# A second accumulator, two pool regions and moved gate and SiLU steps in a diffusion trunk layer

## The chip, the cores and the metric

The kernel runs on one core of a Trainium2 chip. TensorE (PE) multiplies, VectorE (DVE), ScalarE (ACT) and GpSimd (POOL) do the rest, and SyncE (SP) issues the DMAs; each works through its own queue in order, and semaphores join them. The metric is the device time of one execution in microseconds; lower is better. Three runs of the kernel before gave a median of 1373.22 us (1372.56 to 1376.62).

## What is computed

One layer of a trunk for 1024 latent tokens (a grid of 16 rows of 64) and 128 context tokens, model width 1024, float32:

```python
ada = jax.nn.silu(cond) @ p['w_ada'] + p['b_ada']
sh1, sc1, g1, sh2, sc2, g2 = jnp.split(ada, 6, axis=-1)
h = modulate(layer_norm(x), sh1, sc1)
proj = h @ p['w_in']
...
pool_out = pool_mixer(xp.reshape(B, rows, cols, POOL_W), p['w_pool'], p['pool_scale']).astype(x.dtype)
ml_out, st_new = mlstm_mixer(q, k, v, o, gates, p['w_qk_conv'], p['b_gates'], p['hn_g'], st0)
mix = jnp.concatenate([pool_out, ml_out], axis=-1) @ p['w_out']
x = layer_norm(ALPHA * x + g1[:, None, :] * mix, p['ln1_g'], p['ln1_b'])
h = modulate(layer_norm(x), sh2, sc2)
ffn = conv_ffn(h, rows, cols, p['w_up'], p['w_dw'], p['b_dw'], p['w_down'])
x = layer_norm(ALPHA * x + g2[:, None, :] * ffn, p['ln2_g'], p['ln2_b'])
```

The pooling mixer takes, in four groups of 128 channels, means over windows of 2, 4, 8 and 16 in both grid directions, subtracts the input and multiplies each group by a 128 x 128 matrix and a scale. The mLSTM mixer convolves q and k over three tokens, applies SiLU, and scans chunks of 128 tokens forwards and backwards with gates that come from 16 further columns of the projection.

## The kernel before

Each engine has one program. This case is about the stretch from 93 us to 345 us: the input projection and the first step of the scan.

**Units.** The projection up to the scan has 16 tiles of 128 output columns: four of the pooling input, then four of v, of q and of k; four more tiles, of the output gate, follow in units 32 to 39. A tile is two units (halves of the contraction) `n`; a unit is three groups `g` of 384 tokens, each of 12 matmuls, so 36 matmuls. Every weight block is split into a rounded part `whi` (ACT, `hi(n)`) and a rest `wlo` (`lo(n)`: DVE up to unit 25, POOL from unit 26 on), and three products are summed. The two buffers of `whi` and `wlo` alternate, so `hi(n + 2)` waits until unit `n` is done, and PE starts unit `n` when `lo(n)` is done. Tiles 8 to 15 (units 16 to 31) are q and k: when a tile is complete, ACT copies it out of PSUM, DVE adds the two outer taps of the convolution (`conv(j)`, line 2668, four instructions), and ACT applies SiLU (`silu(j)`, line 1729).

**Between the units.** PE's loop over `n` has small jobs in it. `ada2_cols(j)` (line 1145, its matmuls in line 1113) turns modulation block `j` of six into columns in PSUM bank 6. A block is summed by DVE in eight `ada_unit`s of two instructions (lines 2684 and 2686) into the one accumulator `aacc`; the first unit of block `j` waits until the columns of block `j - 1` have been read. The table `ADA_UNITS` says which unit of the projection is followed by how many of them, and `ADA_COLS` follows from it: block 0 is read in unit 5, block 1 in 11, block 2 in 19, block 3 in 27, 4 in 29, 5 in 31, after group 0 of that unit. The gate jobs `gT`, `grow`, `mcol` and `tok` (lines 1212 to 1226) alternate with DVE's `gate_chain1` to `gate_chain5`. After units 10 to 21 one job of four transposes (line 1236) turns v into rows, through PSUM bank 7, and ACT copies it out (`v_evac`, line 1746); after units 24 to 29 come twelve `pool_job`s (line 1248), which multiply the pooled channels by `w_pool`, each into the same columns of bank 7. ACT scales the result into the tile `po` (`po_evac`, line 1723), rounds it to `pohi` (line 1725), POOL forms `polo` (`po_lo`), and SP writes both to DRAM (`spill_pool`). `po_evac(j)` waits for the `polo` of `j - 1`, since `po` is one tile, and from `j = 3` on also for the spill of `j - 3`.

**The pooling mixer** itself, window means of the four groups, is a chain of instructions on POOL (lines 2206 to 2251). It starts when `gate_chain4` is done, and pool job 0 is copied out when it has ended (`pool_y`).

**SP** issues in program order, for each `n`: the block of unit `n + 4`, the loads of `adaw` (two `ada_unit`s to a pair, two buffers, each load waits for the pair before last), then the spills. In the scan, `O_SLOTS` says at which of three places (a, b, c) of a step PE does one group of the output gate's projection.

## Time and profile before

| | |
|---|---|
| median of three runs | 1373.22 us |
| the profiled execution | span 1374.0 us |
| PE busy | 1276.8 us, 93% of the span |
| DVE busy | 1026.9 us, 75% |
| POOL busy | 674.8 us, 49% |
| ACT busy | 589.6 us, 43% |
| PE's waits between 93 us and 345 us | 19.6 us in 9 waits of 0.5 us or more |

The span runs from the first to the last instruction of the profiled execution; the page gives no other time of it. Busy PE is not PE at its peak, since the end of a matmul is modelled.
### The profile page before, as it was taken

How to read it: one execution, taken by the hardware profiler on the slowest of the kernel's cores; microseconds unless marked ns; L12 is line 12 of the kernel's file. 1: busy time of each engine (PE TensorE's matmuls, PEld its weight loads, DVE VectorE, ACT ScalarE, POOL GpSimd, SP SyncE). 2: the span in 40 equal slices, each digit the busy share in tenths (PEclk: the TensorE clock that was granted, in tenths of full speed). 3: DMA queues.
4: the chain of work that ended last, by engine and by line, in shares of the span. 5: the costliest groups of instructions: out<-in, count | busy, mean ns of one | idle time of the engine just before them, and what ended most of it. 6: DMA issues, size and time to landing. Idle time of an engine off the chain costs nothing.

```text
span 1374.0 us, 21762 instructions
## 1 busy us (share of the span) xinstructions
PE 1276.8 (93%) x7739; PEld 1181.1 (86%) x7739; DVE 1026.9 (75%) x1510; ACT 589.6 (43%) x1019; POOL 674.8 (49%) x507
## 2 busy tenths in 40 slices
PE   5899899988999699998799999999999999999995
PEld 3689899878898677898799999999999988888884
DVE  7565669674566688879977778877875689878698
ACT  5442123444435625544344444444443455445420
POOL 1001999333333131227968787978786974300011
PEclk9899899999999799999899999999999999999998
DMA  9432221364235243111253545345444479955774
GB/s 341 144 93 85 66 85 46 107 212 114 82 85 206 84 171 108 62 62 31 90 187 114 189 152 166 134 155 178 141 161 144 158 249 330 351 165 184 239 255 195
DMA packets 164339, 210.28 MB, mean 153 GB/s; under 512 B 10567, under 2 KB 101795, under 8 KB 164003
## 3 DMA queue, kind: packets, MB, share of 16 engines
q1 hardware_dynamic: 163774, 204.47, 45.1%
q0 software_dynamic: 288, 4.72, 0.9%
q8 instruction: 46, 0.75, 0.2%
q14 instruction: 34, 0.28, 0.1%
q10 hardware_dynamic: 197, 0.06, 0.0%
HBM read 161.49 MB, written 47.72 MB: 152 GB/s over the span
## 4 chain that ended last, share of the span: by engine, by line
PE 77%; DVE 10%; issue 3%; ACT 3%; POOL 3%; DMA 3%; SPq 0%; DVEq 0%; POOLq 0%; ACTq 0%
PE ps L1202 12%; PE ps L1548 10%; PE ps L1546 10%; PE ps L1547 10%; PE ps L1581 5%; PE ps L1580 5%; PE ps L1579 5%; PE ps L1154 2%; DMA adaw<-in_w_ada 1%; PE ps L1422 1%; PE ps L1113 1%; PE ps L1424 1%; PE ps L1423 1%; DVE qk L2668 1%; PE ps L1330 1%
## 5 line engine op out<-in xcount | busy, mean ns | idle before, releaser
L2980 DVE SCALAR_TENSOR_TENSOR ps<-gs,taps,ps 128x945 f32<-128x945 f32 (+2 forms) x176 | 215.8, 1226 | 56.9 <-ACT ps L1956 51.5
L1202 PE MATMUL ps<-h1hi,whi 128*128 128x384 f32 x432 | 154.6, 358 | 0.0
L1202 PE MATMUL ps<-h1lo,whi 128*128 128x384 f32 x432 | 147.1, 341 | 0.0
L1202 PE MATMUL ps<-h1hi,wlo 128*128 128x384 f32 x432 | 147.1, 340 | 0.0
L2321 POOL TENSOR_TENSOR rstd<-mv,neghalf 128x1 f32<-128x1 f32 x27 | 27.5, 1018 | 242.1 <-DVE mv L3154 161.5
L1579 PE MATMUL ps<-dwhi,uhi 128*128 128x512 f32 x290 | 113.0, 390 | 1.3 <-POOL dwlo L2173 1.3
L1581 PE MATMUL ps<-dwhi,ulo 128*128 128x512 f32 x290 | 112.8, 389 | 0.0
L1580 PE MATMUL ps<-dwlo,uhi 128*128 128x512 f32 x290 | 112.8, 389 | 0.0
L1546 PE MATMUL ps<-thi,xhi 128*128 128x288 f32 x320 | 96.9, 303 | 8.6 <-issue 5.2
L1548 PE MATMUL ps<-thi,xlo 128*128 128x288 f32 x320 | 96.5, 302 | 0.0
L1547 PE MATMUL ps<-tlo,xhi 128*128 128x288 f32 x320 | 96.5, 302 | 0.0
L2173 POOL TENSOR_TENSOR wlo<-raw,whi 128x512 fp32r<-128x512 f32 x46 | 67.8, 1477 | 56.4 <-ACT whi L1651 27.0
L1546 PE MATMUL ps<-thi,whi 128*128 128x288 f32 x320 | 94.2, 294 | 0.7 <-POOL wlo L2173 0.7
L1548 PE MATMUL ps<-thi,wlo 128*128 128x288 f32 x320 | 94.4, 295 | 0.0
L1547 PE MATMUL ps<-tlo,whi 128*128 128x288 f32 x320 | 94.2, 294 | 0.0
L2686 DVE SCALAR_TENSOR_TENSOR aacc<-adaw,colv,aacc 128x512 f32<-128x512 f32 x84 | 88.9, 1098 | 2.8 <-DMA adaw<-in_w_ada 2.2
L1202 PEld LDWEIGHTS ps<-h1hi,whi 128*128 128x128 f32 x432 | 83.2, 193 | 2.0 <-issue 0.2
L1202 PEld LDWEIGHTS ps<-h1lo,whi 128*128 128x128 f32 x432 | 83.3, 193 | 1.7 <-issue 0.2
L1651 ACT ACTIVATE whi<-raw 128x512 fp32r<-128x512 f32 x42 | 26.3, 628 | 133.9 <-PE ps L1202 132.8
L1202 PEld LDWEIGHTS ps<-h1hi,wlo 128*128 128x128 f32 x432 | 83.0, 192 | 0.0
L1548 PE MATMUL ps<-h2hi,wlo 128*128 128x288 f32 x240 | 71.5, 298 | 0.0
L1546 PE MATMUL ps<-h2hi,whi 128*128 128x288 f32 x240 | 71.4, 297 | 0.0
(425 smaller groups left out, 3998.9 us busy)
## 6 DMA issues: line engine op xcount, KB each, us to landing
raw<-in_w_up SPq DMA_DIRECT2D x78, 256.0 KB, 4.6
u_rows<-val SPq DMA_DIRECT2D x22, 576.0 KB, 2.9
adaw<-in_w_ada SPq DMA_DIRECT2D x24, 512.0 KB, 3.9
st<-in_w_down SPq DMA_DIRECT2D x22, 512.0 KB, 4.4
t_rows<-st SPq DMA_DIRECT2D x11, 1024.0 KB, 5.0
raw<-in_w_in SPq DMA_DIRECT2D x40, 256.0 KB, 4.1
w_raw<-in_w_down SPq DMA_DIRECT2D x33, 256.0 KB, 4.9
v_raw<-u_rows SPq DMA_DIRECT2D x33, 256.0 KB, 4.7
```

What stands on the lines that cost most here:

```text
L1154: last = mm(ps[:, 3 * tile + g, 0:GN], a[:, n % 2, k * P:(k + 1) * P], b[:, kk, grp(g)], start=(kk == 0 and a is whi and b is h1hi), stop= ...
L1202: last = mm(ps[:, bank, 0:GN], a[:, n % 2, k * P:(k + 1) * P], b[:, kk, grp(g)], start=(kk == 0 and a is whi and b is h1hi), stop=(kk == K ...
L1546: mm(out, hi_w[:, ks], b_hi[:, k, cols], start=(n < 2 and k == 0), stop=False, skip_group_check=True)
L1547: mm(out, hi_w[:, ks], b_lo[:, k, cols], start=False, stop=False, skip_group_check=True)
L1548: last = mm(out, lo_w[:, ks], b_hi[:, k, cols], start=False, stop=(k == KH - 1), skip_group_check=True)
L1579: mm(out, u_hi, w_hi, start=start, stop=False, skip_group_check=True)
L1580: mm(out, u_hi, w_lo, start=False, stop=False, skip_group_check=True)
L1581: return mm(out, u_lo, w_hi, start=False, stop=stop, skip_group_check=True)
L2173: return nc.gpsimd.tensor_tensor(out, full, hi_part.bitcast(F32), ALU.subtract)
L2321: tt(rstd[:, j % 4, :], mv[:, j % 4, 1:2], neghalf[:, 0, :], ALU.pow).then_inc(rstd_ready, 1)
L2686: last = stt(out, src, s_col, out, ALU.mult, ALU.add)
L2980: step(stt(a3[:, ro, co], g3[:, ri, ci], taps[:, tap:tap + 1], a3[:, ro, co], ALU.mult, ALU.add), 2 + m)
```

## The change

It does these things:

- A second accumulator `aacc_side`, where no live data lie once two small tables of the gates have been written to DRAM, takes blocks 3 and 5 of the modulation. The first unit of blocks 3, 4 and 5 then waits for the columns of one block earlier than before.
- `ADA_UNITS` has a unit more after projection units 21 and 23 and one less after 27 and 28, so block 3 is read in unit 26 instead of 27.
- The columns of all six blocks are read after group 1 of their unit instead of group 0; from unit 26 on PE waits there until ACT has copied out all pool jobs that lie in bank 6.
- Pool jobs alternate between bank 7 and columns 128 to 511 of bank 6, and `po` is two tiles. A pool job waits for the copy of the job before last, and ACT's copy for the `polo` of the job before last. ACT waits for the spill behind that copy, no longer ahead of it.
- `gate_chain5` moves on DVE from after the units of `n = 9` to ahead of them.
- `silu(j)` moves on ACT from the end of an odd `n` to the end of the even `n` that follows.
- The first group of unit 33 moves from place b of scan step 0 to ahead of the scan.

```diff
-ADA_UNITS = {..., 19: 1, 21: 1,
-             23: 1, 24: 3, 25: 3, 26: 3, 27: 4, 28: 4, 29: 3}
+ADA_UNITS = {..., 19: 1, 21: 2,
+             23: 2, 24: 3, 25: 3, 26: 3, 27: 3, 28: 3, 29: 3}
+ADA_SIDE = (3, 5)
...
-O_SLOTS = {0: "abc", 1: "ac", ...}
+O_SLOTS = {0: "ac", 1: "ac", ...}
...
-        po = place("po", [P, GN], work_at + 4 * 2 * T + 4 * H * P)
+        po = [place("po0", [P, GN], work_at + 4 * 2 * T + 4 * H * P), place("po1", [P, GN], past_xt + 1600)]
...
+        aacc_side = place("aacc_side", [P, 2, AC], tmp_at + 4 * 4 * AC + 8 * AC)
...
+        def ada_sum(blk):
+            return aacc_side if blk in ADA_SIDE else aacc
+
+        def pool_bank(j):
+            return ps[:, 7, 0:GN] if j % 2 == 0 else ps[:, 6, P:P + GN]
...
-                acc_cols(6, 2 * (4 + j) * AB, [aacc[:, w, :] for w in both]).then_inc(pe_ada, 1)
+                acc_cols(6, 2 * (4 + j) * AB, [ada_sum(j)[:, w, :] for w in both]).then_inc(pe_ada, 1)
...
-                if j:
-                    pe.wait_ge(po_ready, j)
-                mm(ps[:, 7, 0:GN], wpl[:, g, :], qk[:, H + g, grp(part)], start=True, stop=True).then_inc(pe_pool, 1)
+                if j >= 2:
+                    pe.wait_ge(po_ready, j - 1)
+                mm(pool_bank(j), wpl[:, g, :], qk[:, H + g, grp(part)], start=True, stop=True).then_inc(pe_pool, 1)
...
-                    if g == 0 and n in ADA_COLS:
+                    if g == 1 and n in ADA_COLS:
+                        if n > POOL_FIRST:
+                            pe.wait_ge(po_ready, min(2 * (n - POOL_FIRST), 12))
                         ada2_cols(ADA_COLS[n])
...
             for g in range(NG):
                 o_unit(U_C, g)
+            o_groups = [(n, g) for n in range(U_C + 1, U_OUT) for g in range(NG)]
+            o_unit(*o_groups.pop(0))
...
                 if j == 0:
                     act.wait_ge(pool_y, 4)
-                else:
-                    act.wait_ge(polo_ready, j)
+                elif j >= 2:
+                    act.wait_ge(polo_ready, j - 1)
+                fn(po[j % 2][:, :], pool_bank(j), ACT.Copy, scale=colv[:, V_PS + g:V_PS + g + 1]).then_inc(po_ready, 1)
+                act.wait_ge(po_ready, j + 1)
                 if j >= 3:
                     act.wait_ge(po_out[r], 32 * g)
-                fn(po[:, :], ps[:, 7, 0:GN], ACT.Copy, scale=colv[:, V_PS + g:V_PS + g + 1]).then_inc(po_ready, 1)
-                act.wait_ge(po_ready, j + 1)
-                fn(pohi[:, r, :], po[:, :], ACT.Copy).then_inc(pohi_ready, 1)
+                fn(pohi[:, r, :], po[j % 2][:, :], ACT.Copy).then_inc(pohi_ready, 1)
...
-                    if 2 * H < tile < NPROJ - 1:
-                        silu(tile - 2 * H - 1)
+                elif 2 * H < n // 2 - 1 < NPROJ - 1:
+                    silu(n // 2 - 2 - 2 * H)
...
                 if kk == 0:
-                    dve.wait_ge(pe_ada, N_ADA1 + blk)
+                    dve.wait_ge(pe_ada, N_ADA1 + (blk if blk < ADA_SIDE[0] else blk - 1))
+                    if blk == ADA_SIDE[0]:
+                        dve.wait_ge(rows_out, 32)
...
-                if n == 10:
-                    gate_chain5()
...
+                if n == 9:
+                    gate_chain5()
                 for unit in range(ada_done(n - 1), ada_done(n)):
                     ada_unit(unit)
```

Line numbers in the order of the changed kernel are 7 to 13 higher than before.

DVE's queue around units 9 and 10. Before, the four instructions on `aacc` (`ada_unit` 14 and 15) stand ahead of `gate_chain5` (the copies into `tok` and `decb`); `wlo<-raw,whi` are `lo(11)` and `lo(12)`:

```order
L2523 TENSOR_TENSOR wlo<-raw,whi 128x512
L2686 SCALAR_TENSOR_TENSOR aacc<-adaw,colv,aacc 128x512 x4
L2645 COPY tok<-ps 128x128
L2646 TENSOR_SCALAR tok<-ps 128x128
L2647 COPY tok<-ps 128x128
L2648 COPY decb<-ps 128x128
```

The same place of the changed kernel:

```order
L2533 TENSOR_TENSOR wlo<-raw,whi 128x512
L2655 COPY tok<-ps 128x128
L2656 TENSOR_SCALAR tok<-ps 128x128
L2657 COPY tok<-ps 128x128
L2658 COPY decb<-ps 128x128
L2661 MEMSET v_75 128x36
L2698 SCALAR_TENSOR_TENSOR aacc<-adaw,colv,aacc 128x512 x4
```

The gate chain has passed the four accumulator instructions.

ACT's queue at units 19 to 21: `whi<-raw` are `hi(21)` and `hi(22)`, the two copies out of `ps` are tile 9, `v_75<-ps` are copies of v, and line 1729 is `silu(0)`. Before:

```order
L1651 ACTIVATE whi<-raw 128x512
L1780 ACTIVATE qk<-ps,colv 128x1152
L1782 ACTIVATE work<-ps 128x1152
L1729 ACT_TABLE_LOAD
L1729 ACTIVATE qk<-qk 128x1152
L1746 ACTIVATE v_75<-ps 128x4x128
L1651 ACTIVATE whi<-raw 128x512
L1746 ACTIVATE v_75<-ps 128x4x128
```

And in the changed kernel:

```order
L1661 ACTIVATE whi<-raw 128x512
L1790 ACTIVATE qk<-ps,colv 128x1152
L1792 ACTIVATE work<-ps 128x1152
L1756 ACTIVATE v_75<-ps 128x4x128
L1661 ACTIVATE whi<-raw 128x512
L1739 ACT_TABLE_LOAD
L1739 ACTIVATE qk<-qk 128x1152
L1756 ACTIVATE v_75<-ps 128x4x128
```

The SiLU now stands behind the next copy of v and the next rounding.

PE's queue in unit 5, with row numbers: the first row each time is the last matmul ahead of the columns of block 0, and line 1113 (1121) is that read. Before:

```order
257 L1202 MATMUL ps<-h1hi_71,wlo_51 128x384
258 L1113 MATMUL ps<-pick_59,aacc_107 128x2 x8
259 L1202 MATMUL ps<-h1hi_71,whi_50 128x384
260 L1202 MATMUL ps<-h1lo_72,whi_50 128x384
261 L1202 MATMUL ps<-h1hi_71,wlo_51 128x384
```

In the changed kernel:

```order
269 L1210 MATMUL ps<-h1hi_71,wlo_51 128x384
270 L1121 MATMUL ps<-pick_59,aacc_108 128x2 x8
271 L1210 MATMUL ps<-h1hi_71,whi_50 128x384
272 L1210 MATMUL ps<-h1lo_72,whi_50 128x384
273 L1210 MATMUL ps<-h1hi_71,wlo_51 128x384
```

The read stands 12 matmuls, one group, later; the `grow` job behind it is row 307 in both.

## Rows read from the trace of the kernel before

**Rows 1.** The page: its first line; the adaw loads: KB each, us to landing.

```profile
span 1374.0 us, 21762 instructions
...
adaw<-in_w_ada SPq DMA_DIRECT2D x24, 512.0 KB, 3.9
```

**Rows 2.** Waits of PE, 93 to 345 us: us in total, times, longest.

```profile
PE ps L1248 <- ACT po L1723: 7.0, 3, 3.5
PE ps L1236 <- DVE decb L2648: 3.9, 1, 3.9
PE ps L1113 <- DVE aacc L2686: 3.5, 1, 3.5
PE ps L1236 <- ACT v L1746: 3.0, 1, 3.0
PE ps L1292 <- ACT qk L1729: 1.0, 1, 1.0
PE ps L1305 <- ACT kw L1812: 0.7, 1, 0.7
```

**Rows 3.** Windows after two waits: length, busy times, granted clock, DMA share, GB/s.

```profile
145.00:158.50 13.50, 13.50 (x58) 13.47 (x59) 5.13 (x4) 0.60 (x1) 12.86 (x12) 0.62 0.27 78
279.00:284.00 5.00, 4.35 (x14) 3.70 (x13) 4.96 (x6) 3.52 (x5) 2.68 (x2) 0.66 0.92 308
```

**Rows 4.** Timelines of PE and DVE, units 5 and 6: start, duration, instruction, idle before.

```profile
101.77 1.84 PE L1113 MATMUL ps<-pick,aacc 128*128 128x2 f32 x16
...
112.18 0.60 PE L1217 MATMUL ps<-ident,gcol 128*1 128x128 f32 x4
...
103.72 0.88 DVE L2684 TENSOR_SCALAR aacc<-adaw,colv 128x512 f32<-128x512 f32 x2 [2.59 <-PE ps L1113]
...
111.96 0.17 DVE L2611 MEMSET mrow<- 1x128 f32 x1
```

**Rows 5.** Timeline of DVE, unit 10.

```profile
135.77 8.26 DVE L2686 SCALAR_TENSOR_TENSOR aacc<-adaw,colv,aacc 128x512 f32<-128x512 f32 x4
```

**Rows 6.** Timeline of ACT, unit 20.

```profile
220.71 1.16 ACT L1729 ACTIVATE qk<-qk 128x1152 f32<-128x1152 f32 x1 [3.69 <-DVE qk L2668]
```

**Rows 7.** Timeline of DVE, units 18 to 24.

```profile
205.51 2.67 DVE L2523 TENSOR_TENSOR wlo<-raw,whi 128x512 fp32r<-128x512 f32 x1 [4.46 <-ACT whi L1651]
...
220.60 0.68 DVE L2523 TENSOR_TENSOR wlo<-raw,whi 128x512 fp32r<-128x512 f32 x1
...
227.23 7.21 DVE L2668 SCALAR_TENSOR_TENSOR qk<-work,colv,qk 128x1023 f32<-128x1023 f32 x4
...
234.97 3.79 DVE L2686 SCALAR_TENSOR_TENSOR aacc<-adaw,colv,aacc 128x512 f32<-128x512 f32 x2
...
241.49 3.32 DVE L2668 SCALAR_TENSOR_TENSOR qk<-work,colv,qk 128x1023 f32<-128x1023 f32 x4
244.72 0.69 DVE L2523 TENSOR_TENSOR wlo<-raw,whi 128x512 fp32r<-128x512 f32 x1
```

**Rows 8.** Timeline of PE: first matmul of unit 25.

```profile
249.08 0.64 PE L1202 MATMUL ps<-h1hi,whi 128*128 128x384 f32 x1
```

**Rows 9.** Timeline of POOL: first step of the mixer, equal steps of its first and last group, last step.

```profile
130.96 1.29 POOL L2211 MEMSET poolA<- 128x1424 f32 x1 [51.51 <-DVE enm L2641]
...
144.42 2.37 POOL L2250 TENSOR_TENSOR qk<-poolB,qk 128x1024 f32<-128x1024 f32 x1
...
238.28 2.73 POOL L2250 TENSOR_TENSOR qk<-poolB,qk 128x1024 f32<-128x1024 f32 x1
241.09 0.79 POOL L2251 TENSOR_TENSOR qk<-poolA,qk 128x128 f32<-128x128 f32 x1
```

**Rows 10.** Waits of DVE (93 to 330 us) and of SP's queue (120 to 345 us).

```profile
DVE aacc L2684 <- PE ps L1113: 25.3, 5, 10.8
...
SPq L729 <- DVE aacc L2686: 114.9, 15, 16.2
```

More of the change, by code:

```diff
@@ L95 @@
 ADA_FIRST = 8
-ADA_UNITS = {4: 2, 6: 2, 7: 1, 8: 1, 9: 2, 10: 1, 11: 1, 12: 1, 13: 1, 14: 1, 15: 1, 16: 1, 17: 1, 18: 1, 19: 1, 21: 1,
-             23: 1, 24: 3, 25: 3, 26: 3, 27: 4, 28: 4, 29: 3}
+ADA_UNITS = {4: 2, 6: 2, 7: 1, 8: 1, 9: 2, 10: 1, 11: 1, 12: 1, 13: 1, 14: 1, 15: 1, 16: 1, 17: 1, 18: 1, 19: 1, 21: 2,
+             23: 2, 24: 3, 25: 3, 26: 3, 27: 3, 28: 3, 29: 3}
+ADA_SIDE = (3, 5)
 def ada_done(n):
@@ L112 @@
 GRP_ORDER = (1, 0, 2)
-O_SLOTS = {0: "abc", 1: "ac", 2: "ac", 3: "ac", 4: "abc", 5: "abc", 6: "abc", 7: "abc"}
+O_SLOTS = {0: "ac", 1: "ac", 2: "ac", 3: "ac", 4: "abc", 5: "abc", 6: "abc", 7: "abc"}
 O_HI = {0: 34, 1: 35, 3: 36, 4: 37, 5: 38, 6: 39, 7: 40, 8: 41}
@@ L1364, in h_transposes @@
                 hT[0] += 1
-            o_groups = [(n, g) for n in range(U_C + 1, U_OUT) for g in range(NG)]
             def o_slot(s, name):
@@ L2257, in po_lo @@
                     pool.wait_ge(po_out[r], 32 * g)
-                sub_hi(polo[:, r, :], po[:, :], pohi[:, r, :]).then_inc(polo_ready, 1)
+                sub_hi(polo[:, r, :], po[j % 2][:, :], pohi[:, r, :]).then_inc(polo_ready, 1)
             def lo(n):
@@ L2679, in ada_unit @@
                 if kk == 0:
-                    dve.wait_ge(pe_ada, N_ADA1 + blk)
+                    dve.wait_ge(pe_ada, N_ADA1 + (blk if blk < ADA_SIDE[0] else blk - 1))
+                    if blk == ADA_SIDE[0]:
+                        dve.wait_ge(rows_out, 32)
                 for w, v0 in enumerate((V_C, V_CC)):
-                    src, s_col, out = adaw[:, pair % 2, u % 2, :], colv[:, v0 + kk:v0 + kk + 1], aacc[:, w, :]
+                    src, s_col, out = adaw[:, pair % 2, u % 2, :], colv[:, v0 + kk:v0 + kk + 1], ada_sum(blk)[:, w, :]
                     if kk == 0:
```

## The prediction

> **What bounds the kernel now.** I read the page first: the span [rows 1], in which PE is busy 93%. What PE waits for is the next view, cut to the stretch that the change touches: six kinds of wait, 19.1 us in all [rows 2]. Then the granted clock in windows around them, the timelines of the queues that end the waits, and last the waits of DVE and SP. The reader is to see that PE sets the pace of this stretch, that each wait is a short queue effect on another engine, and that idle PE is paid twice: after the 3.9 us wait the clock stood at 0.62 over 13.5 us, so 13.5 x 0.38 = 5.1 us more were lost, and after the 3.5 us wait at 279 us it stood at 0.66 over 5 us, 1.7 us more [rows 3]. From there the clock was 1.2 GHz until PE had been busy for a while, then 2.4 GHz.
>
> Units are counted as in the section on the kernel. All of it lies before the scan, and nothing behind the scan is touched, so what the start of the scan gains, the end gains.
>
> **Part by part.** I follow PE through the stretch and keep the sum of what it is ahead.
>
> (a) Columns of a block one group later. Block 0's read took 1.84 us from 101.77 and the `grow` job began at 112.18, four groups later [rows 4]: (112.18 - 103.61) / 4 = 2.1 us a group. DVE had waited for that read, began the next accumulator unit at 103.72, and went through the gate chain to the memset at 111.96 that releases `grow` [rows 4]; PE came 0.1 us behind. With the read one group later, DVE and ACT shift by 2.1 us, but PE arrives at `grow` at the same time, since read and group only change places. A new wait of 2.1 us: **ahead -2.1**. The mixer on POOL, which started when DVE's chain released it at 130.96 [rows 9], starts 2.1 us later too.
>
> (b) `gate_chain5` first. PE's job behind unit 10 waited 3.9 us for it [rows 2], as it stood behind four accumulator instructions of 8.26 us [rows 5]. It now runs right behind `lo(11)`, 5 us before PE needs it. Wait and half clock go: 3.9 + 5.1 = 9.0. Those four instructions end 3.0 us later than before (the chain's 0.9 and the 2.1), at 147.0; PE needs them for block 1's columns at 147.8, now that the read stands one group later. Cover 0.8 us; they ran beside the mixer, at 4.1 us a pair, and if one of them takes half as long again, that cover is gone and PE waits for the rest, about 1 us. **Ahead 6.9.**
>
> (c) SiLU behind the copy of v. `silu(0)` waited until 220.71 for the convolution [rows 6], and PE 3.0 us for the copy of v behind it [rows 2]. The copy now finds ACT free. But `lo(21)`, which PE needs next, stood behind the same convolution on DVE and ended at 221.28 [rows 7]: DVE is late next. Its queue from `lo(20)` on starts 6.9 us earlier, at 198.6, and takes 221.28 - 205.51 - 0.5 (its wait for the columns of block 2, which the second accumulator ends) = 15.3 us, so `lo(21)` lands at 213.9, 1.0 us after PE asks. Gain 2.0: **ahead 8.9**.
>
> (d) One more accumulator unit ahead of `lo(24)`. Here DVE is full. From 205.51 to the start of `conv(2)` at 241.49 it took 36.0 us [rows 7]; without the 0.5 and with one unit more, at 3.8 us as the last one took [rows 7], 39.3: `lo(24)` at 237.9. PE started unit 24 right behind it, at 241.9; 8.9 us ahead it would start at 233.0. So it waits 5 us in two or three pieces (0.6 at unit 23, 3.6 at unit 24, by the same sum), and is **ahead 3.7** when it starts, 0.3 us behind `lo(24)`. `conv(2)` ran in 3.3 us because the mixer ended at 241.89; beside the mixer `conv(1)` took 7.2 [rows 7, 9]. Now it starts at 237.9 beside the mixer, so `lo(25)` comes at about 245.9 against 245.41 before. PE began unit 25 at 249.08 [rows 8], so it is **ahead 3.1** there. The extra unit is bounded below by 1.7 us (3.79 x 3.32 / 7.21, the convolution's ratio of quiet to not) and above by 4.1 (half of 8.26 [rows 5]); I take 3.8, its own neighbour.
>
> (e) The mixer's end. It ended at 241.89 [rows 9]. It starts 2.1 us later, and DVE is dense beside it some 7 us longer; equal steps took 2.37 us in the first group and 2.73 in the last [rows 9], 15%, so add 1: 245.0. Pool job 0 is then copied by 245.6; job 2 in unit 25 asks at 248.0. Nothing is lost, with 2.4 us of cover.
>
> This is where a rule speaks against the change. DVE's convolution took 7.2 us beside the mixer and 3.3 without it [rows 7]. The Trainium skill (SBUF — State Buffer, Who interferes with whom) says that a DVE instruction with two SBUF inputs and a GpSimd instruction that reads SBUF exclude each other for the whole instruction. The trace agrees for DVE; for POOL the 15% are far less than full exclusion. By the rule the mixer would lengthen by all DVE work that is new beside it; that is the second rival.
>
> (f) From unit 25 to the scan. The three waits for `po` (7.0), the one for block 5 (3.5), the one at the scores (1.0) and the one for `kw` (0.7) [rows 2] go, with two lapses of the clock, 1.7 each [rows 3], where the one behind the wait at 312 us is taken as alike: 15.6. Two regions and two tiles take ACT's copy and POOL's subtraction off PE's path: a job now needs the copy before last, at least 4 us old. The wait at 279 us was ACT's for a spill that SP had not issued, because SP's queue waited for DVE, 16.2 us at the longest [rows 10], and DVE for block 3's columns, 10.8 us [rows 10]. With the side accumulator DVE goes on, and ACT waits for the spill behind the copy that PE needs. Is DVE in time for the last block? From 246 us it has 20 units, at 1.7 to 2.1 us, and four convolutions at 3.3: 47 to 55 us. Two buffers, a landing of 3.9 us [rows 1] and 3.4 us for a pair on DVE allow a pair each 3.7 us, 37 us for ten, so DVE's own work bounds it: it ends at 293 to 301. PE asks at 298. Cover 5 us to none. The new wait for ACT's copies ahead of a block's columns finds them 1.5 us or more old. The first group of unit 33 takes 2.1 us wherever it is; ahead of the scan it hides the last SiLU and the table load, and what it no longer hides in step 0, DVE's division before the second numerators, costs between 0.3 us and 1.2; I take 0.4, near the short wait for the same release in later steps. **Ahead 3.1 + 15.6 - 0.4 = 18.3.**
>
> **The sum** is against the span of 1374.0 us; the median is 0.8 us below it and nothing else lies around it, so I carry the difference to the median: 1373.2 - 18.3 = 1354.9.
>
> **Rivals.**
>
> 1. DVE is not late. If the extra unit and `conv(2)` cost what they cost with POOL quiet (1.7 and 3.3), (d) loses 1 to 2 us instead of 5.8, and the time is 1373.2 - 22.6 = about 1350. For it: single `lo` steps took 0.68 us even beside the mixer [rows 7], so DVE is not always slowed. Against: the convolution took 7.21 against 3.32 [rows 7].
>
> 2. The mixer pays in full. New beside it are one unit (1.7), `conv(2)` (3.3) and `lo(25)` (0.7), quiet lengths: 5.7. It ends at 241.9 + 2.1 + 5.7 = 249.7, its first copy at 250.3, so PE waits 2.3 us at job 2, and 1.3 us more of DVE's work is beside it. If the clock also falls after the 3.6 us wait at unit 24, as it did after 3.5 [rows 3], 1.7 more: 1358 to 1360.
>
> 3. The feed does not run ahead. If DVE needs 2.0 us a unit or the spills hold SP up, the wait for block 5's columns comes back, 3.5 us and 1.7 of clock: 1360.
>
> 4. Slower than before. One mechanism: DVE and the mixer stretch each other. The mixer's end holds job 2, hence unit 25 and all behind it, one for one. It took 110.9 us [rows 9]; it decides from an end at 266 us, 21 us past my 245.0, a stretch of 19% of the whole mixer. At 270 us the wait would be long enough to lower the clock as well: 1380. Against it: the last group, which had DVE at its densest, shows 15% on its own steps only.
>
> 5. The change doesn't do what it says: DVE stays tied to PE's reads in spite of the side accumulator, because the first unit of block 5 still waits for block 3's columns. Then half of (f) stays: 1362.
>
> **Chances.** Forecast (1352 to 1357) 0.48; rival 1 0.17; rival 2 0.14; rival 3 0.09; rival 4 0.05; rival 5 0.07. Leaving out rival 4, rival 5 and the tail of rival 3 and of rival 1 gives 1348 to 1361. What this kernel's measurement can tell from no change is about 0.3%, 4.1 us. Below 1369 lie all but rival 4 and the tail of rival 5: faster 0.91, same 0.04, slower 0.05.
>
> **What would show it.** In PE's waits: a new one of about 2 us at `grow`; none at the v job behind unit 10, and clock 1.00 there; at units 21, 23 and 24 waits for `wlo` of DVE of 1.0, 0.6 and 3.6; none for `po`, none for block 5's columns; scores straight behind unit 33's first group, at about 308.7. In POOL's timeline a mixer from 133 to 245. In ACT's, `po_evac(6)` waits for a DMA between its copy and `pohi`. The prediction is wrong if the mixer ends past 248, if the waits for `wlo` sum to over 8 us or under 2, or if a wait opens behind the scan.

## Result, and the profile after

The changed kernel took 1360.88 us, median of four runs (1357.80 to 1366.34), against 1374.37 for the kernel before on the same chip: 0.9906 of it, 95% interval 0.9885 to 0.9927. That is faster, by 13 us and not by the 18 that were forecast: above the 1352 to 1357 to which the forecast gave its largest chance, and at the very top of the wider range, 1348 to 1361. The execution in the trace of the changed kernel took 1357.80 us, 1.7 us more than its span; it is the fastest of the four.

The page of the changed kernel, its first line and PE's busy time:

```profile
span 1356.1 us, 21771 instructions
...
PE 1267.9 (93%) x7739; PEld 1173.6 (87%) x7739; DVE 1035.3 (76%) x1510; ACT 588.4 (43%) x1019; POOL 681.8 (50%) x507
```

PE's waits of the changed kernel in the same stretch as [rows 2] (us in total, times, longest):

```profile
PE ps L1210 <- DVE wlo L2533: 3.0, 1, 3.0
PE ps L1121 <- DVE aacc_side L2698: 3.0, 1, 3.0
PE ps L1225 <- DVE mrow L2621: 2.2, 1, 2.2
PE ps L1358 <- DVE Cs L2797: 1.0, 2, 0.5
PE ps L1342 <- DVE hacc L2778: 0.7, 2, 0.4
PE ps L1210 <- POOL wlo L2183: 0.3, 1, 0.3
```

Of the six rows of [rows 2] five are gone; the sixth, the 3.5 us for block 5's columns, is now 3.0, for `aacc_side`. Two of over 1 us are new: 2.2 us at `grow` and 3.0 us for `lo(24)`.

The windows right behind these three waits (length, busy times, granted clock, DMA share, GB/s; as [rows 3]):

```profile
113.70:117.10 3.40, 3.40 (x12) 3.40 (x12) 0.00 (x0) 0.00 (x0) 0.00 (x0) 0.51 0.31 82
...
236.50:240.00 3.50, 3.50 (x12) 2.89 (x11) 3.46 (x3) 0.00 (x0) 3.42 (x2) 0.52 0.30 82
...
301.50:308.30 6.80, 6.80 (x25) 6.80 (x25) 2.31 (x6) 0.94 (x2) 0.23 (x1) 0.50 0.35 98
```

Behind every one of them the clock stood at its lower level, 1.2 GHz: 3.4, 3.4 and 6.8 us long, in which PE does half of its work. Together that costs 6.8 us; the forecast had none of it.

Where the time went is best seen from the start of the units. All numbers are us from PE's first matmul of unit 4, read from PE's timeline; "end of scan" is PE's first matmul behind the scan.

| | unit 7 | 12 | 21 | 24 | 25 | 32 | end of scan |
|---|---|---|---|---|---|---|---|
| before | 21.8 | 65.6 | 129.8 | 148.7 | 156.0 | 226.6 | 378.4 |
| changed | 25.5 | 60.4 | 121.5 | 143.7 | 152.7 | 215.4 | 365.5 |
| ahead | -3.7 | 5.2 | 8.3 | 5.0 | 3.3 | 11.2 | 12.9 |
| forecast | -2.1 | 6.9 | 8.9 | 3.7 | 3.1 | 17.0 | 18.3 |

(The forecast at unit 32 is its 3.1 at unit 25, the waits of 7.0 and 3.5, and 3.4 of clock.) The spans differ by 17.9 us: the 12.9, 1.4 us ahead of unit 4, and 3.6 us behind the scan, where no step was changed. A second profile of the same kernel, below, has 12.1 instead of 12.9. What lies behind the scan took between 898.2 and 902.4 us in the fourteen traces of this document, so the 3.6 us are scatter and no part of the effect.

DVE of the changed kernel from `conv(2)` on (start, duration, instruction, idle before):

```profile
235.25 7.23 DVE L2678 SCALAR_TENSOR_TENSOR qk<-work,colv,qk 128x1023 f32<-128x1023 f32 x4
242.40 0.68 DVE L2533 TENSOR_TENSOR wlo<-raw,whi 128x512 fp32r<-128x512 f32 x1
243.00 11.17 DVE L2698 SCALAR_TENSOR_TENSOR aacc_side<-adaw,colv,aacc_side 128x512 f32<-128x512 f32 x8
...
256.03 3.95 DVE L2678 SCALAR_TENSOR_TENSOR qk<-work,colv,qk 128x1023 f32<-128x1023 f32 x4
...
270.50 1.41 DVE L2698 SCALAR_TENSOR_TENSOR aacc<-adaw,colv,aacc 128x512 f32<-128x512 f32 x2 [0.97 <-DMA adaw<-in_w_ada]
271.94 5.55 DVE L2678 SCALAR_TENSOR_TENSOR qk<-work,colv,qk 128x1023 f32<-128x1023 f32 x4
...
288.12 1.42 DVE L2698 SCALAR_TENSOR_TENSOR aacc_side<-adaw,colv,aacc_side 128x512 f32<-128x512 f32 x2 [1.59 <-DMA adaw<-in_w_ada]
289.57 5.55 DVE L2678 SCALAR_TENSOR_TENSOR qk<-work,colv,qk 128x1023 f32<-128x1023 f32 x4
295.05 5.34 DVE L2698 SCALAR_TENSOR_TENSOR aacc_side<-adaw,colv,aacc_side 128x512 f32<-128x512 f32 x6
300.42 3.13 DVE L2678 SCALAR_TENSOR_TENSOR qk<-work,colv,qk 128x1023 f32<-128x1023 f32 x4
```

DVE no longer waits for PE here, as it did for 10.8 us in [rows 10]; but its last unit of block 5 ends at 300.4, and PE had asked for that block's columns at 297.5. Three convolutions that were priced at 3.3 us took 3.95, 5.55 and 5.55, though the mixer had ended: what POOL does in this time is `polo` and `lo(n)`.

The mixer itself, its first and last step on POOL (as [rows 9]), and ACT's wait between a pool job's copy and its `pohi`:

```profile
133.24 1.29 POOL L2221 MEMSET poolA<- 128x1424 f32 x1 [55.18 <-DVE enm L2651]
...
245.42 0.79 POOL L2261 TENSOR_TENSOR qk<-poolA,qk 128x128 f32<-128x128 f32 x1
```

```profile
ACT pohi L1735 <- DMA pool_out<-polo: 18.7, 4, 8.4
```

It took 113.0 us against 110.9, from 133 to 246. ACT's waits for the spills, 18.7 us in four, are all behind the copy that PE needs; no wait of PE names them.

### The profile page after: what moved, and what is told of

It reads as the page before. It is cut to its first block, busy times and chain, and to the rows that moved or that the text cites. A ratio compares the mean times of both kernels' runs of the same rounds, so it can differ in the third digit from the quotient of the medians.

```text
span 1356.1 us, 21771 instructions
## 1 busy us (share of the span) xinstructions
PE 1267.9 (93%) x7739; PEld 1173.6 (87%) x7739; DVE 1035.3 (76%) x1510; ACT 588.4 (43%) x1019; POOL 681.8 (50%) x507
## 4 chain that ended last, share of the span: by engine, by line
PE 77%; DVE 10%; POOL 4%; issue 3%; ACT 3%; DMA 3%; SPq 0%; DVEq 0%; POOLq 0%; ACTq 0%
PE ps L1210 13%; PE ps L1558 11%; PE ps L1556 10%; PE ps L1557 10%; PE ps L1589 5%; PE ps L1591 5%; PE ps L1590 5%; PE ps L1162 2%; DMA adaw<-in_w_ada 1%; DVE qk L2678 1%; PE ps L1432 1%; PE ps L1434 1%; PE ps L1433 1%; DVE aacc_side L2698 1%; PE ps L1487 1%
## 5 line engine op out<-in xcount | busy, mean ns | idle before, releaser
L2183 POOL TENSOR_TENSOR wlo<-raw,whi 128x512 fp32r<-128x512 f32 x46 | 71.0, 1545 | 50.5 <-ACT whi L1661 21.1
L1556 PEld LDWEIGHTS ps<-thi,xhi 128*128 128x128 f32 x320 | 61.5, 192 | 13.0 <-ACT ps L2062 7.1
```

The lines of the kernel that those rows point to most:

```text
L1556: mm(out, hi_w[:, ks], b_hi[:, k, cols], start=(n < 2 and k == 0), stop=False, skip_group_check=True)
L2183: return nc.gpsimd.tensor_tensor(out, full, hi_part.bitcast(F32), ALU.subtract)
```

## Experiments

Every ratio below is against the kernel before on the same chip, with its 95% interval. The kernel before had medians of 1372.79 us (beside the runs with the small `polo`, the gate chain put back, the old table and block 0), 1375.76 (the SiLU, one region, one accumulator and the first spread of the units), 1375.25 (the change again, the gate chain alone and the second spread) and 1374.74 (the short mixer). An interval is 2 to 4 us to either side, so two ratios are clearly apart only from some 4 us on; smaller parts rest on the traces, one for each kernel. "Ahead", "earlier" and "later" are again read from the unit starts counted from unit 4.

Three parts of the change were never undone by themselves: the second `po` tile together with the wait for the spill behind ACT's copy, the later read of the blocks other than block 0, and the place of unit 33's first group.

### The change again

> The changed kernel itself, for its distance from before and a second trace. The stretch from unit 4 to the end of the scan is 365.5 us in its first trace and 378.4 before: if that stretch is the whole effect, the time is 12 to 14 us below before, and the rest of the kernel (898.8 and 902.4 us in the two traces) lies between 898 and 903 in every trace. If the rest is part of the effect, it is 3 us or more shorter again.

1359.89 us (1358.45 to 1363.81), 0.9904 (0.9881 to 0.9927); span 1358.4. The same waits in the same places (2.2, 3.0, 3.0) and the same three lapses of the clock, 3.4, 3.4 and 6.8 us. The stretch to the end of the scan took 366.3 us and the rest 899.8, so the stretch is the whole effect. The result stands, and so do its waits: they are no accident of one execution.

### What stretches DVE behind unit 25

```diff
-                sp.dma_start(pool_out[1, :, g, grp(r)], polo[:, r, :].bitcast(F32)).then_inc(po_out[r], 16)
+                sp.dma_start(pool_out[1, :, g, grp(r)], pohi[:, r, :].bitcast(F32)).then_inc(po_out[r], 16)
...
-                sub_hi(polo[:, r, :], po[j % 2][:, :], pohi[:, r, :]).then_inc(polo_ready, 1)
+                sub_hi(polo[:, r, 0:1], po[j % 2][:, 0:1], pohi[:, r, 0:1]).then_inc(polo_ready, 1)
```

> The changed kernel with the POOL subtraction that makes the low part of the pooled channels cut from 384 columns to 1; the spill of the low part takes the rounded part instead. Left out: the low part of the pooling mixer's output. Theory A (VectorE is late for block 5 because POOL's subtractions stretch its units): its stretch from the low part of unit 25 to the last unit of block 5, 57 us now, falls to 50 or less, the 3.0 us wait for block 5's columns goes and half clock at 301 us with it: 4 to 6 us below the changed kernel. Theory B (it is late because of the loads of the modulation weights and their place in the queue): the stretch stays at 55 us or more and the wait stays.

1355.56 us, 0.9869 (0.9848 to 0.9889). POOL's and DVE's groups, POOL from 245 to 310 us and DVE from 243 to 302 (busy, mean ns | idle before), of the changed kernel:

```profile
L2183 POOL TENSOR_TENSOR polo<-po,pohi 128x384 fp32r<-128x384 f32 x12 | 17.3, 1444 | 21.4 <-ACT pohi L1735 21.4
...
L2698 DVE SCALAR_TENSOR_TENSOR aacc<-adaw,colv,aacc 128x512 f32<-128x512 f32 x14 | 13.1, 974 | 1.1 <-DMA adaw<-in_w_ada 1.0
```

and of this kernel:

```profile
L2183 POOL TENSOR_TENSOR polo<-po,pohi 128x1 fp32r<-128x1 f32 x12 | 6.5, 544 | 16.9 <-ACT pohi L1735 16.9
...
L2698 DVE SCALAR_TENSOR_TENSOR aacc<-adaw,colv,aacc 128x512 f32<-128x512 f32 x14 | 10.1, 761 | 1.5 <-DMA adaw<-in_w_ada 1.4
```

The same fourteen accumulator instructions fell from 974 to 761 ns. DVE's first and last units of the stretch in this kernel:

```profile
246.44 9.14 DVE L2698 SCALAR_TENSOR_TENSOR aacc_side<-adaw,colv,aacc_side 128x512 f32<-128x512 f32 x8
...
289.22 5.22 DVE L2698 SCALAR_TENSOR_TENSOR aacc_side<-adaw,colv,aacc_side 128x512 f32<-128x512 f32 x6
```

The stretch took 48.0 us instead of 57.4 (243.0 to 300.4 in the change). The twenty units took 34.2 us instead of 39.8 and the three convolutions 10.4 instead of 15.1, while DVE's waits in it, nearly all for loads, grew from 2.6 to 3.5. The wait for block 5's columns was gone, with its 6.8 us of half clock, and unit 32 began at 208.9 instead of 215.4, 6.5 us earlier: 3.0 of the wait and 3.4 of the clock. This shows what made DVE late: theory A. The loads are not the cause by themselves, since their waits stayed and PE did not wait.

### What each cover of the forecast was worth

**The SiLU** back at its old place:

```diff
-                elif 2 * H < n // 2 - 1 < NPROJ - 1:
-                    silu(n // 2 - 2 - 2 * H)
+                    if 2 * H < tile < NPROJ - 1:
+                        silu(tile - 2 * H - 1)
```

> The changed kernel with each SiLU back at the end of the odd n. Theory A (waits are worth their length): the 3.0 us wait at the v job behind unit 20 comes back and stays, 3 us above the changed kernel. Theory B (VectorE paces units 21 to 24): PE waits 2 to 3 us at unit 21 instead of 3.0 us at unit 24; less than 1 us above.

1362.42 us, 0.9899 (0.9883 to 0.9916). PE's waits:

```profile
PE ps L1121 <- ACT po L1731: 3.3, 1, 3.3
PE ps L1225 <- DVE mrow L2621: 2.2, 1, 2.2
PE ps L1210 <- DVE wlo L2533: 2.2, 1, 2.2
...
PE ps L1244 <- ACT v L1756: 0.7, 1, 0.7
```

The wait for v came back with 0.7 us only, unit 21 was 0.9 us later, and the one for `lo(24)` was 0.8 shorter. New is 3.3 us at block 3's columns, for ACT's copy of a pool job, with 10.2 us of half clock behind it: the wait that the change adds ahead of a block's columns can bind. But the wait for block 5 was gone and unit 32 began 1.3 us later than in the change. Neither theory has this course: the wait for v was short, and the one at unit 24 did not go. As a ratio the edit can't be told from nothing.

**One region of bank 7**, two `po` tiles kept:

```diff
-            return ps[:, 7, 0:GN] if j % 2 == 0 else ps[:, 6, P:P + GN]
+            return ps[:, 7, 0:GN]
...
-                if j >= 2:
-                    pe.wait_ge(po_ready, j - 1)
+                if j >= 1:
+                    pe.wait_ge(po_ready, j)
```

> The changed kernel with all pool jobs in bank 7 again, each waiting for the copy of the job before it; the two po tiles and ScalarE's order stay. Theory A (the second PSUM region is what took ScalarE's copy off PE's path): waits of 4 to 7 us in sum for po come back at units 26 to 28 with one lapse of the clock, though a part takes the place of the wait for block 5's columns: 2 to 6 us above the changed kernel. Theory B (it was the spill wait behind the copy and the second tile): waits of 1 us at most, time the same.

1360.42 us, 0.9888 (0.9861 to 0.9916), the time of the change itself. PE's first three waits:

```profile
PE ps L1256 <- ACT po L1731: 4.7, 3, 2.9
PE ps L1210 <- DVE wlo L2533: 3.0, 1, 3.0
PE ps L1225 <- DVE mrow L2621: 2.2, 1, 2.2
```

4.7 us of waits for `po` are back, and nothing is lost: PE comes to block 5's columns that much later, finds them ready, and the only lapse of the clock in the stretch is one of 3.4 us. Unit 32 began at 212.3, 3.1 us earlier than in the change, of which 1.6 is the lapse at `grow` that did not come this time. The waits are those of theory A, the time is that of theory B: the second region is worth nothing measurable while DVE sets the end.

**One accumulator**, all else kept:

```diff
-            return aacc_side if blk in ADA_SIDE else aacc
+            return aacc
...
-                    dve.wait_ge(pe_ada, N_ADA1 + (blk if blk < ADA_SIDE[0] else blk - 1))
-                    if blk == ADA_SIDE[0]:
-                        dve.wait_ge(rows_out, 32)
+                    dve.wait_ge(pe_ada, N_ADA1 + blk)
```

> The changed kernel with all six blocks in the one accumulator and the old waits. Theory A (the second accumulator lets VectorE run ahead, and that is most of the gain behind unit 25): VectorE stands 5 us or more for block 3's columns and again for block 4's, the wait for block 5's columns grows from 3.0 to 8 us or more; 5 to 9 us above the changed kernel. Theory B (the two regions and tiles give that gain): VectorE waits, PE does not, within 2 us of the changed kernel.

1369.58 us, 0.9946 (0.9926 to 0.9966), the time of theory A. Its largest waits of PE by kind, the sum of DVE's waits for PE's reads, and the first unit of block 3:

```profile
PE ps L1210 <- DVE wlo L2533: 8.9, 2, 6.1
PE ps L1210 <- POOL wlo L2183: 2.7, 1, 2.7
```

```profile
DVE aacc L2694 <- PE ps L1121: 28.5, 5, 13.5
```

```profile
206.04 6.21 DVE L2694 TENSOR_SCALAR aacc<-adaw,colv 128x512 f32<-128x512 f32 x2 [4.57 <-PE ps L1121]
```

DVE waits 28.5 us for PE's reads again (25.3 in [rows 10]), and the work so held back stands ahead of `lo(n)` later. The path is not the one theory A had: block 5's columns cost PE 1.4 us, not 8 or more. 6.4 us are lost already at unit 21, where the first convolution and `lo(21)` stand behind block 3's first unit. That unit waited 4.57 us for block 2's columns, and 2.48 us in the run below that moves only the gate chain; the difference is the length of one group, by which the change reads the columns later. So a part of what the second accumulator brings only pays for the later read. By the two ratios it carries 5.5 us of the 13 (with intervals of 3 us either way); by the two traces the scan ends 10.4 us later without it. It is the largest of the parts that were undone, in either view.

### What the gate chain brings, undone and alone

```diff
+                if n == 10:
+                    gate_chain5()
...
-                if n == 9:
-                    gate_chain5()
```

> The changed kernel with the fifth gate chain put back behind the accumulator units of n = 10. Theory A (each wait that went is worth its own length): the 3.9 us wait behind unit 10 and its 5.1 us of half clock come back and nothing else moves, so 9 us above the changed kernel, about 1370. Theory B (VectorE paces units 18 to 31, so an earlier PE mostly waits for it later): PE is 9 us later at unit 12, but the third convolution then runs partly after the mixer, and the wait for block 5's columns shrinks from 3.0 to 0 to 1.5 us, its half clock with it: 2 to 6 us above, 1363 to 1367.

1360.77 us, 0.9912 (0.9891 to 0.9933). PE's waits:

```profile
PE ps L1210 <- DVE wlo L2533: 5.0, 3, 3.1
PE ps L1244 <- DVE decb L2658: 3.9, 1, 3.9
PE ps L1225 <- DVE mrow L2621: 2.2, 1, 2.2
```

The 3.9 us are back (with 3.4 us of half clock this time, not 10.2), unit 12 is 5.5 us later than in the change and unit 25 9.1, but unit 32 only 2.2 and the end of the scan 1.8: the wait for block 5 is gone. This is the course of theory B, though its time of 1363 to 1367 was too high by 2 us or more. Seven of nine microseconds were given back at the last wait, since DVE, not PE, decides when it ends.

The opposite edit, on the kernel before: `gate_chain5` ahead of the units of `n = 9` and nothing else.

> The kernel before with the fifth gate chain ahead of the units of n = 9 and nothing else. Theory A (the wait and its half clock are worth their length): 9 us below before. Theory B (a good part is given back where VectorE and the mixer's end set the pace): a wait of about 1 us for block 1's columns, PE 8 us ahead at unit 12 and 6 at unit 25, all later waits as before: 5 to 7 us below before.

1375.57 us, 1.0006 (0.9987 to 1.0026): nothing, where both theories had 5 us or more. Its waits of PE, then of DVE:

```profile
PE ps L1248 <- ACT po L1723: 13.4, 4, 6.9
PE ps L1113 <- DVE aacc L2686: 4.0, 2, 3.5
PE ps L1236 <- ACT v L1746: 1.3, 1, 1.3
```

```profile
DVE aacc L2684 <- PE ps L1113: 26.9, 5, 14.0
```

Unit 24 began 9.7 us ahead of the kernel before, unit 25 only 2.2. Between them stands a new wait of 6.9 us for `po`, and 6.8 us of half clock behind it. ACT's copy of pool job 0 waited for the mixer, and the mixer ended later, not earlier; POOL's last row:

```profile
244.15 0.78 POOL L2251 TENSOR_TENSOR qk<-poolA,qk 128x128 f32<-128x128 f32 x1
```

It started at 130.64 and took 114.3 us (110.9 in [rows 9]). Behind unit 25 the last 2.2 us went as well, and unit 32 began 1.7 us later than before: the lapses at 278 and 312 us were 6.8 us long each, not 3.4. To tell the mixer from DVE behind it, the same kernel with a shorter mixer:

```diff
+                if g < 2:
-                link(tt(mid, res, bc(invt[:, g, 0:GRID_H]...
-                link(tt(res, mid, bc(invt[:, g, GRID_H:GRID_H + GRID_W]...
+                    link(tt(mid, res, bc(invt[:, g, 0:GRID_H]...
+                    link(tt(res, mid, bc(invt[:, g, GRID_H:GRID_H + GRID_W]...
```

> The kernel before with gate_chain5 ahead of the units of n = 9, as in the run that made this one edit alone and gained nothing (unit 24 began 9.7 us earlier, unit 25 only 2.2), and with a shorter mixer: groups 2 and 3 leave out their two multiplications of 128x1024 with the table of counts (2.77 and 2.90 us in that run), so the mixer ends some 11 us earlier and the pooled values of these groups are not divided. Theory A (the 9 us of the gate chain were given back at the mixer's end: POOL ended at 244.9, PE had to wait 6.9 us at a pool job for it, and its clock was at half for 6.8 us behind that): the wait of 6.9 is gone, unit 25 begins 8 to 10 us earlier, at 144 to 146 us after unit 4, and of that 6 us or more last to the scan, since behind unit 25 the same waits stand as before: 1366 to 1369 us. Theory B (behind unit 25 DVE with its one accumulator sets the pace, and no earlier mixer helps): the wait for po goes, but the waits for the columns of blocks 3 to 5 grow by as much, unit 32 begins no more than 2 us earlier, and the time is 1372 to 1376 us.

1369.32 us (twelve runs), 0.9966 (0.9953 to 0.998), by the two ratios 5.5 us below the run without the cut, and between the times of the two theories. The mixer ended at 232.1, and the 6.9 us wait and its lapse were gone: PE had stood there for the mixer, as A says. That the whole gain would have come without that wait is not shown. Unit 25 came only 3.2 us ahead of before, not 10, and 1.0 us ahead of the run with the whole mixer; at the end of the scan it was 4.1. Another wait had grown:

```profile
PE ps L1248 <- ACT po L1723: 7.0, 3, 3.7
PE ps L1236 <- ACT v L1746: 4.6, 1, 4.6
```

The v job behind unit 20 now waits 4.6 us instead of 1.3, behind `silu(0)`, which waits for `conv(0)` on DVE. Why DVE was late there is in single rows; the two below account for 3.6 us, and the accumulator pair behind them took 5.24 us instead of 1.26. `lo(20)` on DVE and POOL's add beside it, in this kernel:

```profile
199.31 4.29 DVE L2524 TENSOR_TENSOR wlo<-raw,whi 128x512 fp32r<-128x512 f32 x1 [2.83 <-ACT whi L1651]
...
199.03 4.02 POOL L2228 TENSOR_TENSOR poolB<-poolA 128x1792 f32<-128x1792 f32 x1
```

and in the run with the whole mixer:

```profile
197.15 0.69 DVE L2523 TENSOR_TENSOR wlo<-raw,whi 128x512 fp32r<-128x512 f32 x1 [2.90 <-ACT whi L1651]
...
197.16 2.91 POOL L2250 TENSOR_TENSOR qk<-poolB,qk 128x1024 f32<-128x1024 f32 x1
```

The same DVE instruction takes 0.69 us when it starts just ahead of a POOL instruction, and 4.29 when it starts 0.28 us behind one: it ends 0.55 us after POOL's. The Trainium skill (SBUF — State Buffer, Who interferes with whom) states that issue order, not the shape of the operation, decides who blocks; these rows agree for DVE.

### Where the two costs of the change lie

**The old table of units**, the rest of the change kept:

```diff
-ADA_UNITS = {..., 19: 1, 21: 2,
-             23: 2, 24: 3, 25: 3, 26: 3, 27: 3, 28: 3, 29: 3}
+ADA_UNITS = {..., 19: 1, 21: 1,
+             23: 1, 24: 3, 25: 3, 26: 3, 27: 4, 28: 4, 29: 3}
```

> The changed kernel with the old table of accumulator units (one after units 21 and 23, four after 27 and 28); the second accumulator stays. Theory A (the wait for the weights' low part at unit 24 costs its 3.0 us at the end): that wait goes and the time falls by 3, to about 1358. Theory B (VectorE's total work up to the last unit of block 5 decides): the wait at unit 24 goes, but the one for block 5's columns grows from 3.0 to about 6 us; time the same within 1 us.

1357.34 us, 0.9882 (0.9862 to 0.9903), some 3 us better than the change by the medians, though the intervals overlap. That is theory A's time, but not its course, nor B's. PE's first wait:

```profile
PE ps L1256 <- ACT po L1731: 5.1, 1, 5.1
```

`lo(24)` is not waited for and unit 25 begins at 147.8, 4.9 us earlier than in the change. PE then comes to a pool job ahead of the mixer's end and waits 5.1 us, with 6.8 us of half clock. Block 5 is not waited for, though DVE has more to do there: unit 32 at 211.6.

**Block 0's columns** again after group 0 of unit 5:

```diff
-                    if g == 1 and n in ADA_COLS:
+                    if g == (0 if n == 5 else 1) and n in ADA_COLS:
```

> The changed kernel with block 0's columns read after group 0 of unit 5 as before; the other blocks stay after group 1. Theory A (the new 2.2 us wait at the grow job comes from this alone and is on the path): the wait falls to 0.1 and the time by 2.1 us; the mixer starts 2.1 us earlier. Theory B (later waits for VectorE absorb it): the wait goes, but the waits at unit 24 and for block 5's columns grow by as much in sum; time the same.

1357.22 us, 0.989 (0.9868 to 0.9912); the interval overlaps that of the change. The wait at `grow` and its lapse were gone: unit 7 was at 21.8 and units 12 to 25 3.6 to 3.7 us ahead of the change, so 2.2 of wait and 1.5 of clock. At unit 32 2.1 of it were left, and 1.6 at the end of the scan: PE waited 3.0 us for block 5 again, and 1.2 instead of 0.3 for POOL's `lo` just ahead of it. So most of the wait was on the path, as theory A has it, and about 2 of the 3.7 us were given back later.

**Units spread earlier**, where PE leaves DVE time, with block 0 read as just above:

```diff
-ADA_UNITS = {..., 12: 1, 13: 1, 14: 1, 15: 1, 16: 1, 17: 1, 18: 1, 19: 1, 21: 2,
-             23: 2, 24: 3, 25: 3, 26: 3, 27: 3, 28: 3, 29: 3}
+ADA_UNITS = {..., 12: 1, 13: 2, 14: 1, 15: 2, 16: 1, 17: 2, 18: 1, 19: 1, 21: 1,
+             23: 1, 24: 3, 25: 3, 26: 3, 27: 3, 28: 3, 29: 2}
```

> The changed kernel with block 0 read after group 0 and three accumulator units moved to units 13, 15 and 17, out of 21, 23 and 29. If VectorE beside the mixer is what is left: unit 24's wait of 3.0 us goes, the wait for block 5's columns goes too, and the scores come 8 to 10 us earlier than in the changed kernel (3.7 of them from block 0): about 1351. The rival: the mixer's end, through pool job 2 in unit 25, takes the place of both: a wait of 3 to 5 us there with half clock behind it, and the time is 1356 to 1358.

1353.07 us (1350.42 to 1356.69), 0.9827 (0.9805 to 0.9849): faster than both kernels. PE's largest wait:

```profile
PE ps L1210 <- DVE wlo L2533: 5.0, 1, 5.0
```

It stands ahead of unit 21, behind the first convolution, which took 11.9 us beside the mixer:

```profile
205.86 11.92 DVE L2678 SCALAR_TENSOR_TENSOR qk<-work,colv,qk 128x1023 f32<-128x1023 f32 x4
```

It has 6.8 us of half clock behind it, and neither theory had it. The waits at unit 24 and for block 5 are gone, and pool job 2 is not waited for. PE has no other wait of over 1 us in the stretch; unit 32 at 207.9, end of the scan at 358.3, 20.1 us ahead of before and 7.2 of the change.

A second spread of the units, meant to take away these 5 us as well:

```diff
-ADA_UNITS = {..., 12: 1, 13: 2, 14: 1, 15: 2, 16: 1, 17: 2, 18: 1, 19: 1, 21: 1,
-             23: 1, 24: 3, 25: 3, 26: 3, 27: 3, 28: 3, 29: 2}
+ADA_UNITS = {..., 12: 2, 13: 1, 14: 2, 15: 1, 16: 2, 17: 1, 19: 1, 21: 1,
+             23: 1, 24: 3, 25: 3, 26: 3, 27: 3, 28: 3, 29: 3}
```

> As the kernel with three units moved to 13, 15 and 17, but the early units are spread so that VectorE is free when the first convolution comes: two after 12, 14 and 16, none after 18, one after 21 and 23, three from 24 to 29. If the 5.0 us wait at unit 21 came from the units right ahead of the first convolution, it falls below 2 us and the clock stays up: 3 to 6 us below that kernel, 1347 to 1350. The rival: the work beside the mixer is the same in sum, so a wait of 3 us or more opens at unit 24 or at pool job 2 instead, and the time stays at 1353.

1354.98 us, 0.9868 (0.9844 to 0.9891), no better than the first. PE's waits:

```profile
PE ps L1256 <- ACT po L1731: 5.9, 1, 5.9
...
PE ps L1210 <- DVE wlo L2533: 0.6, 1, 0.6
```

The wait for `wlo` fell to 0.6, unit 25 began 7.1 us earlier (144.9 against 152.0), and all of it was spent waiting for the mixer, 5.9 us and 6.8 us of half clock, as the rival says. By these waits the mixer's end is what holds PE next; an earlier or shorter mixer was not tried with this table.

## Why the prediction was wrong

- **The step that failed is the last cover of (f)**, "Cover 5 us to none" for block 5's columns. It was none: PE waited 3.0 us, and the lapse behind took 3.4 more. From 243.0 to 300.4 DVE worked 57.4 us, where the text had 47 to 55. The units were right, 20 in 39.8 us (1.99 each, within the 1.7 to 2.1). The convolutions were not: 15.1 us for the three that lie ahead of the last unit, where 3.3 each gives 9.9; the fourth, counted too, runs behind it. And two waits for loads, 0.97 and 1.59, had been counted as none. The 3.3 us had been read where POOL was quiet; `polo` and `lo(n)` stretch DVE as the mixer does, which the run with the small `polo` showed: there the same stretch took 48.0 us and PE did not wait for block 5. Rival 3, given 0.09, had this outcome (3.5 + 1.7 there, 3.0 + 3.4 here) but not its cause: with 1.99 us a unit and 3.3 a convolution DVE would have been done at 292.7, ahead of PE.
- **No wait was priced with a lapse of its own in the sum.** It credits 5.1 and 3.4 us for lapses that end, and sets none against the waits that it adds. They came behind all three: 1.7 at `grow`, 1.7 at unit 24, 3.4 at block 5. From unit 25 to unit 32 the forecast had 13.9 us of gain and 7.9 came; the 3.0 us of wait and 3.4 of clock at block 5 are about that difference.
- (a) 2.1 us was 2.2, at `grow`, as said. With the clock it cost 3.7; the run that undid it gave 3.7 back at units 7 to 25.
- (b) was right at its place: the wait of 3.9 and 10.2 us of half clock went, and unit 12 was 5.2 ahead, 6.9 less the lapse of (a). As a saving of the kernel it was over-valued: undone it cost 1.8 us at the end of the scan (0.8 by the ratios), alone it brought nothing.
- (c) The order of events was right, the size not shown: ahead 8.3 at unit 21 against 8.9, without the waits of 1.0 and 0.6 for `wlo`; undone it cost 0.9 us at unit 21.
- (d) One wait of 3.0 instead of 0.6 and 3.6 (which add up to 4.2, where the sum itself uses 5.2); `lo(24)` at 235.3, not 237.9, of which 1.4 us is this trace's earlier start of unit 4; `conv(2)` took 7.2 beside the mixer, as said. Ahead 5.0 and 3.3 at units 24 and 25, against 3.7 and 3.1.
- (e) 246.2 against 245.0, and no wait for it. The nearness is partly luck: counted from unit 4, the mixer ended 5.7 us later than before, not 3.1, since it began 3.7 later with the lapse of (a), and took 2.1 longer instead of 1. The rule of full exclusion (the Trainium skill, SBUF — State Buffer, Who interferes with whom) had been worked out to 249.7; the mixer paid 2.1 us for the DVE work that came beside it, not 5.7. In three runs in which PE came earlier the mixer's end was the next bound, with waits of 5.1, 5.9 and 6.9 us. Rival 2 had a wait at that place, but from a mixer that pays in full, which no run showed: it never took more than 114.7 us.
- The three waits for `po` and the two for the scan's first operands went, and ACT waited for the spills behind its copy, as said.
- None of the three signs of being wrong came: the mixer ended ahead of 248, the waits for `wlo` of DVE were 3.0 us in sum, and no wait opened behind the scan in both profiles of the change. They watched parts (d) and (e); the part that failed, (f), had no such sign, only a line in the list of what to see.

## What to carry to other kernels

A chain of waits on three engines has to be walked to its end before gains are added: here the gate chain's 9 us were worth 0 alone and at most 2 in the change, since most of them were given back at the mixer's end in the one and at DVE's last unit in the other, while the second accumulator, which unties DVE from PE's reads, was worth 5.5 to 10. A duration read where the neighbour engine was quiet is a lower bound, not a mean, for a stretch where it works. And each wait that an edit adds or uncovers should be priced with a lapse of the clock behind it, as those that it removes are.

## What the hardware showed

- Length of wait and length of lapse go loosely together. The 3.9 us wait for `decb` had 10.2 us of half clock behind it in the kernel before and 3.4 in the run that put the chain back. The 3.0 us wait for v in the kernel before had none; 3.0 us for `lo(24)` in the change had 3.4; 2.2 us at `grow` had 3.4 in both profiles of the change, and none in the run with one region, in which it was 2.2 us too. One lapse of 3.4 us is worth 1.7 by the granted clock (1.6 at unit 7, from the runs with and without it), so by estimate two kernels with equal waits can differ by some 3 us in this stretch alone.
- One `lo` instruction on DVE takes 0.69 or 4.29 us, by whether it starts a moment ahead of or behind a long POOL instruction. The traces show this as a rule with hardly an exception. In 95 cases a `lo` of DVE began beside the mixer while a two-operand POOL instruction (TENSOR_TENSOR) had more than 0.2 us left; 94 times it ended 0.55 us behind that instruction, to within 0.01 us, and the 95th, which began within 0.01 us of POOL's, took 0.69. Beside a MEMSET of POOL with 0.76 us or more left, in four cases, it took 0.69. So a shift of a microsecond ahead can move DVE's work by several. That this alone made 4.6 us out of the wait of 1.3 is argued, not shown.
- The mixer, always the same instructions, took 110.4 to 114.7 us over the runs that left it whole, a spread of 4%; while one convolution on DVE took up to 9.0 us beside it in the change, 11.9 in the first spread of the units, and 3.1 without it. In these runs most of the cost of the conflict fell on DVE.
